# Moving a unit's product with the values two quarters into the next unit, in a one-core attention and convolution layer

## What is computed

```python
hn = rmsnorm(x, norm_w)
q, k, v, g_attn, h, c_gate, b_gate, g_conv = split(hn @ w_in)
attn = swa_sink_attention(q, k, v, sinks, rel_bias)   # 16 heads of 64, 2 key/value heads,
                                                      # chunks of 64 queries by 128 keys
conv = b_gate * causal_conv3(c_gate * h)
mixed = concat([attn * silu(g_attn), conv * silu(g_conv)])
out = rmsnorm(x + mixed @ w_out, final_norm_w)
```

## Time and profile before

| | before |
|---|---|
| median of 3 runs | 1329.38 us (1329.08 to 1330.24) |
| the profiled execution | 1330.21 us |
| its span, first to last instruction | 1328.3 us |
| granted TensorE clock | 0.999 |
| VectorE, ScalarE, GpSimd busy | 71%, 51%, 22% |
| attention on TensorE (L2083, first to last start) | 410.9 to 953.3 us |

### The profile page before, as it was taken

The page is one execution under the profiler, slowest core; times in us unless marked ns, Lnnn a source line. Parts: engine busy times, 40 slices in busy tenths (PEclk is TensorE's granted clock), DMA queues, the critical chain, the costliest instruction groups (busy, mean ns, idle before and its releaser), DMA issues.

```text
span 1328.3 us, 16340 instructions
## 1 busy us (share of the span) xinstructions
PE 1311.7 (99%) x5846; PEld 1082.0 (81%) x5846; DVE 943.9 (71%) x1089; ACT 681.3 (51%) x955; POOL 295.2 (22%) x215
## 2 busy tenths in 40 slices
PE   9999999999999999999999999999999999999997
PEld 7887888888888888888888788877888888888886
DVE  6899766324479569995699956899548896665376
ACT  7856432322235766766656666666623444322444
POOL 1222221000003334333333433533201121110001
PEclk9999999999999999999999999999999999999999
DMA  9779995988887999779997689877898788899778
GB/s 369 285 275 371 386 356 161 310 314 300 326 274 235 313 308 299 220 221 330 320 306 246 223 287 342 248 240 238 304 385 307 287 276 286 305 302 363 266 260 301
DMA packets 168912, 390.00 MB, mean 294 GB/s; under 512 B 79968, under 2 KB 91264, under 8 KB 147200
## 3 DMA queue, kind: packets, MB, share of 16 engines
q1 hardware_dynamic: 149296, 322.08, 70.7%
q0 software_dynamic: 18240, 62.92, 12.9%
q10 hardware_dynamic: 1296, 3.96, 0.8%
HBM read 294.18 MB, written 98.93 MB: 296 GB/s over the span
## 4 chain that ended last, share of the span: by engine, by line
PE 75%; DVE 15%; issue 6%; ACT 2%; POOL 1%; DMA 1%; DVEq 0%; POOLq 0%; ACTq 0%
PE banks L2040 72%; DVE w_ring L1375 3%; DVE raw L1473 2%; DVE x_main L1388 1%; DVE raw L1467 1%; DMA x_park<-e 1%; POOL total L912 1%; PE banks L2000 1%; DVE pt_lo L1636 1%; DVE logits L1605 1%; DVE o_mix L1644 0%; DVE probs L1614 0%; DVE raw L1485 0%; DVE total L1621 0%; DVE e L1681 0%
## 5 line engine op out<-in xcount | busy, mean ns | idle before, releaser
L2040 PE MATMUL banks<-x_main,w_ring 128*128 128x512 f32 x2352 | 547.9, 391 | 0.8 <-DVE e L1536 0.6
L2040 PEld LDWEIGHTS banks<-x_main,w_ring 128*128 128x128 f32 x2352 | 439.8, 188 | 93.6 <-issue 1.4
L991 ACT ACTIVATE w_ring<-raw 128x1024 fp32r<-128x1024 f32 x223 | 235.5, 1056 | 418.7 <-PE banks L2040 415.4
L2040 PE MATMUL banks<-x_far,w_ring 128*128 128x512 f32 x1680 | 390.9, 390 | 2.1 <-DVE e L1533 1.2
L1375 DVE TENSOR_TENSOR w_ring<-raw,w_ring 128x1024 fp32r<-128x1024 f32 x223 | 272.8, 1223 | 164.7 <-ACT w_ring L991 163.2
L2040 PEld LDWEIGHTS banks<-x_far,w_ring 128*128 128x128 f32 x1680 | 314.5, 188 | 69.2 <-ACT e L1115 1.8
L2040 PE MATMUL banks<-w_ring,x_main 128*128 128x512 f32 (+1 forms) x1020 | 230.9, 387 | 0.3 <-DVE e L1533 0.3
L2040 PEld LDWEIGHTS banks<-w_ring,x_main 128*128 128x128 f32 x1020 | 189.9, 188 | 39.6 <-DVE e L1533 0.7
L906 POOL PARTITION_ALL_REDUCE top<-logits x32 | 87.9, 2748 | 365.6 <-DVE logits L1605 365.6
L912 POOL PARTITION_ALL_REDUCE total<-probs x32 | 116.7, 3646 | 155.3 <-ACT probs L1165 155.3
L1022 ACT ACTIVATE x_main<-z 128x512 fp32r<-128x512 f32 x104 | 64.9, 624 | 116.2 <-issue 92.8
(11 more groups left out here) (169 smaller groups left out, 962.7 us busy)
## 6 DMA issues: line engine op xcount, KB each, us to landing
x_far<-x_park SPq DMA_DIRECT2D x84, 1024.0 KB, 7.1
x_main<-x_park SPq DMA_DIRECT2D x84, 1024.0 KB, 6.5
raw<-in_w_blocks_dram SPq DMA_DIRECT2D x127, 512.0 KB, 5.9
x_park<-x_main POOLq DMA_DIRECT2D x104, 512.0 KB, 5.7
q_cur<-qkv_park SPq DMA_DIRECT2D x64, 128.0 KB, 5.5
z<-mix_park SPq DMA_DIRECT2D x16, 512.0 KB, 7.6
z<-in_x_dram SPq DMA_DIRECT2D x6, 1024.0 KB, 12.7
x_park<-e POOLq DMA_DIRECT2D x8, 512.0 KB, 6.1
```

The lines of the kernel that those rows point to most:

```text
L991: act.activation(w_ring[:, n % NW, :, 0, :], raw[:, c, k:k + 2, :], ACT.Copy).then_inc(w_hi_ready, 1)
L2040: op = pe.matmul(bank, left, right, start=(first and i == 0), stop=(kt == HK - 1 and i == 2), skip_group_check=goes_on)
```

## The change

Each call of the attention's tail goes to a later quarter of the next unit; no instruction is added or taken away.

```diff
@@ SyncE
-                    elif o == 3:
+                    elif o == 6:
                         if 0 < u <= UNITS:
                             store_o(u - 1)
                         if u < UNITS:
                             load_g(u)
@@ ScalarE
                     if o == 1 and 0 < u <= UNITS:
+                        invert_total(u - 1)
+                    if o == 3 and 0 < u <= UNITS:
                         move_o_lo(u - 1)
-                        invert_total(u - 1)
-                    elif 0 <= u < UNITS:
-                        if o == 2 and u % 2 == 0:
+                    if 0 <= u < UNITS:
+                        if o == 3 and u % 2 == 0:
                             turn_v(u // 2)
@@ VectorE
-                        elif o == 3 and u % 2 == 0:
-                            turn_v_lo(u // 2)
                         elif o == 4:
                             shift_logits(u)
                         elif o == 7:
                             split_p_lo(u)
+                            if u % 2 == 0:
+                                turn_v_lo(u // 2)
                         elif o == 11:
                             add_sink(u)
-                    if o == 3 and 0 < u <= UNITS:
+                    if o == 5 and 0 < u <= UNITS:
                         weight_gate(u - 1)
                         gate_output(u - 1)
@@ TensorE
-                if o == 0 and 0 < u <= UNITS:
+                if o == 2 and 0 < u <= UNITS:
                     probs_by_values(u - 1)
```

## The result

| | before | after |
|---|---|---|
| median | 1329.38 us (1328.95 to 1330.24, 7 runs) | 1333.51 us (1332.08 to 1334.10, 7 runs) |
| ratio to before, 95% interval | | 1.0027 (1.0018 to 1.0037) |
| the profiled execution, its span | 1330.21, 1328.3 us | 1334.10, 1332.2 us |
| granted TensorE clock, mean | 0.999 | 0.996 |
| VectorE, GpSimd busy | 943.9, 295.2 us | 951.5, 288.2 us |

What follows compares the result with a forecast made beforehand. TensorE, busy 99% of the span, was taken as the bound; 5.98 us of stops less 0.2 at 739, 0.2 at 926 and 0.2 for new brushes gave 5.4 us won: 1324.0 us, range 1322.8 to 1327.3.

Steps and rivals of the forecast that it cites:

- The seven stops: TensorE's waits in the attention: two for ScalarE's copy, four for `pt_lo`, one for a sum; 5.98 us winnable in all.
- ScalarE's part: Output copies moved behind two tile copies: 0.66 + 0.11 us won at 436, 0.77 less 0.2 at 926.
- The 1.1 us at 881: TensorE's wait for `pt_lo` there, 1.10 us, goes with the later product; the 1.21 won stay.
- the 0.67 at 917: TensorE's product with the values, 0.67 us late for `pt_lo`, no longer waits once it comes two quarters later.
- So I take 1.1 us of lead and not 1.75. Bounds: 0 and 1.75.: VectorE at 677.74: other operations fill its 1.75 us wait for ScalarE's `turn_v`, but the shift needs the maximum.
- Some 0.7 us less loss for each unit in a late stretch. Bounds: 0 ... and 1.9.: VectorE beside the reduction: two adds reading bank 5 run on, so 0.85 us of the 1.92 hold costs nothing.
- I take the 1.33 + 0.11 as won save 0.2: TensorE's wait near 739 us for VectorE's sum: lead and smaller holds end that sum before TensorE wants it.
- A stop was priced at its length and 0.11: Each TensorE stop costs its lost time plus 0.11 us for the slower first product behind it; 0.77 in all.
- VectorE stays as late as it is: Rival: VectorE's lead and the saving in holds come to nothing; 2.55 us won, 1326.8 us; chance 0.20.
- The slower rival: GpSimd's reductions starve beside gapless VectorE operations; if all seven in the late stretches do, 1333 us; chance 0.05.
- The fourth copy: Rival: in four passes ScalarE's fourth tile copy comes 1 us past due, 4 us given back; 1328.0 us; chance 0.07.
- The hold: VectorE's two-SBUF-operand operation is held by a reduction, 1.92 us lost; rival whole-instruction blocking makes it 1.1 dearer, chance at most 0.05.

Runs made afterwards that it cites:

- One gate back: Changed kernel with only unit 14's gate, in step 107, back at quarter 3 (o 3), the other 31 at o 5: 1329.33 us.
- the gate at o 8: Changed kernel with VectorE's gate at quarter 8 instead of 5, its store and load at quarter 10: 1325.92 us.
- the stop forced in the kernel before: Kernel before, with TensorE's second tile of step 120 also waiting for the fourth tile's sum of the pass before: 1334.09 us.
- the gate at o 4: Changed kernel with VectorE's gate at quarter 4 instead of 5, still behind the shift but ahead of the tile's sum: 1327.46 us.
- the product back: Changed kernel with TensorE's product with the values back at quarter 0 instead of 2, all else as changed: 1331.53 us.
- the shift behind the gate: Changed kernel with the shift of the logits moved from quarter 4 to 5, behind the gate: 1326.69 us.
- the product at o 1: Changed kernel with the gate at quarter 8, store and load at 10, and the product with the values at quarter 1 instead of 2: 1326.18 us.
- o 9: Changed kernel with VectorE's gate at quarter 9 instead of 5, its store and load at quarter 11: 1326.78 us.

## Why the prediction was wrong, point by point

- **The seven stops.** Right as to what TensorE would no longer wait for. ScalarE's part was right in full: the second tile follows without a gap in the rows at 434.62 and 928.88. The 1.1 us at 881 and the 0.67 at 917 did not come back either.
- **"So I take 1.1 us of lead and not 1.75. Bounds: 0 and 1.75."** This step failed, in its size and in its bounds. The wait for `v_cur` went, and the wait of 1.68 us for the maximum took its place. The list of waits after has a row that the one before did not have:

```profile
DVE probs L1615 <- POOL top L906: 21.8, 13, 1.7
```

  Worse, the bounds held no loss. The step looked at the idle time at 677.74 alone and not at the one in which the old gate ran, 660.35, where VectorE gives 3 us away by program order. The lead was -2.7 us at unit 16. One gate back in its place returned it (2.5 us late instead of 4.9).
- **"Some 0.7 us less loss for each unit in a late stretch. Bounds: 0 ... and 1.9."** Failed in its sign. The holds moved from the weights' sums onto the gate's multiplication and `w_lo`. The gate's multiplication before and after:

```profile
L1648 DVE TENSOR_TENSOR o_mix<-o_mix,g_cur 128x256 f32<-128x256 f32 x32 | 13.6, 426 | 1.1
```

```profile
L1649 DVE TENSOR_TENSOR o_mix<-o_mix,g_cur 128x256 f32<-128x256 f32 x32 | 31.1, 972 | 1.1
```

  That is 17.5 us more, and the low parts (L1375, then L1376) rose by 7.1 us, from 272.8 to 279.9; the sums of weights in L1467, L1473 and L1485 fell by 16.9, from 150.1 to 133.2. VectorE's whole busy time rose by 7.6 us; with the gate at o 8 it is 944.5 us, as before. The lower bound, 0 if the gate's last multiplication takes the whole hold, named the right case but had no room for a loss.
- **"I take the 1.33 + 0.11 as won save 0.2"** followed from these two terms and became 4.0 lost at the same step.
- **A stop was priced at its length and 0.11.** For long ones that is wrong: 2.7 us came on top, as the stop forced in the kernel before shows as well.
- **The rivals.** "VectorE stays as late as it is" had the right mechanism and too small a price, since it let VectorE be as late as before at worst. The slower rival named the reductions of the sum and their starvation. That did not happen: the longest of them takes 4.2 us instead of 8.8, and GpSimd's busy time fell from 295.2 to 288.2 us. Two reductions of the maximum did grow, from 4.15 to 4.96 us at 519 and from 2.68 to 3.82 at 678, and behind both of them the shift waits 1.68 us. The harm lay in what VectorE does beside them. The fourth copy never became the wait.
- **The hold.** A `w_lo` inside a reduction takes 3.26 us against 1.22, 2.04 us of a reduction of 3.28 us. This goes with the reading of the earlier trace rows. The Trainium skill, page "SBUF — State Buffer", section "Who interferes with whom", calls the shared ports an exclusive lock, and says of VectorE's two-port modes that the loser is blocked for the whole instruction. The row at 737.72 disagrees with that reading as well: blocked until the reduction's end at 740.89, the low part would have ended at 742.11, not 740.98.

**The stop at 530 us** (1.5 us) goes with a wait of the shift, too. After:

```profile
519.37 4.96 POOL L906 PARTITION_ALL_REDUCE top<-logits  x1 [8.26 <-DVE logits L1606]
...
524.36 0.69 DVE L1615 SCALAR_TENSOR_TENSOR probs<-top,logits 128x512 f32<-128x512 f32 x1 [1.68 <-POOL top L906]
```

In the kernels that have this stop (after, the gate at o 4, the product back, one gate back: 1.2 to 1.5 us) the maximum's reduction at 519 takes 4.95 us or more, and the shift at 524 waits 1.68 us for it with the gate behind it. With the shift behind the gate the reduction is as long, the shift waits 0.07 us and the stop is 0.2. In the other kernels with the product at o 1 or o 2 the shift does not wait, and there is no such stop. Why that reduction takes 4.95 us in some kernels and 2.68 or 4.15 in others stays open. So do the 2.1 us by which the kernel with the product back at o 0 is slower than before: the moves of ScalarE's calls and of the values were not taken apart from the gate's there.

## What to carry to other kernels

When a call is moved in the program order of an engine that waits elsewhere, ask what idle time it fills now, and not only which wait it leaves: behind a wait for a slower engine, the same 1.56 us are on the list instead of beside it. Removing small waits of the bounding engine removes nothing if another engine's list sets when it can go on; the lateness then adds up to one stop, and where the clock falls behind a long stop that is dearer than the sum of the small ones. If idle time cannot be read to either side of the move, the bounds of the lead must include a loss.

## What was not expected of the hardware

The half clock behind a stop. With a stop of 4.0 us the granted clock is 0.54 and 0.60 in the two stretches of 4 us from 740, and 2.7 us are lost beyond the stop (forced in the kernel before: 0.51 and 0.63). With stops of 1.9 us, as in the kernels with the gate at o 8 and o 9 and with the product at o 0 (at 706), none follows. The stop of 2.0 us in the kernel with one gate back was followed by it, with 1.8 us lost. What else decides between these was not tried.
